# Decode keys of a paged attention turned by VectorE in 32x32 blocks and scored in 16 tiles of the array, with four gate units moved from the prompt's slots to the decode's

## The reference, cut to what matters

```python
s = jnp.einsum('bthd,bnhd->bhtn', q, k_mean)         # block scores (mean key of 256 rows)
_, idx = lax.top_k(s, 3)
s_sel = jnp.einsum('bthd,bhtkld->bhtkl', q, k_sel) * scale
p = softmax(concat([s_sel, s_own]))
out = einsum(p_sel, v_sel) + einsum(p_own, v_own)
u = sigmoid(ga) * (att @ w_attn_br) + sigmoid(gm) * (ml @ w_mlstm_br)
```

## Time and profile before

| | us |
|---|---|
| median of 3 runs (1178.22 to 1182.13) | 1180.7 |
| the profiled execution's own time | 1177.61 |
| its span, first to last instruction | 1175.9 |
| PE busy in the span | 1077.4 (92%) |
| PE weight loads busy | 921.2 (78%) |
| DVE busy | 569.0 (48%) |
| ACT busy | 448.5 (38%) |
| POOL busy | 119.2 (10%) |

### The profile page before, as it was taken

The page is one execution under the profiler, slowest core; times in us unless marked ns, Lnnn a source line. Parts: engine busy times, 40 slices in busy tenths (PEclk is TensorE's granted clock), DMA queues, the critical chain, the costliest instruction groups (busy, mean ns, idle before and its releaser), DMA issues.

```text
span 1175.9 us, 21203 instructions
## 1 busy us (share of the span) xinstructions
PE 1077.4 (92%) x7577; PEld 921.2 (78%) x7577; DVE 569.0 (48%) x1227; ACT 448.5 (38%) x1002; POOL 119.2 (10%) x225
## 2 busy tenths in 40 slices
PE   2999999998999889999989892899999999999993
PEld 2988876887888667777778782898899899889983
DVE  3253524653665565555646427545344334444435
ACT  5154213332554365555543226233133113313312
POOL 2001210220000122333230000000000000000000
PEclk8899989999999999999999997899999999999997
DMA  4432215324114789999974421222222222222312
GB/s 135 141 104 71 54 37 119 80 63 140 50 47 116 259 272 325 339 313 324 314 209 123 160 81 36 72 81 83 81 72 88 80 80 80 84 79 73 96 54 80
DMA packets 93702, 149.81 MB, mean 127 GB/s; under 512 B 9377, under 2 KB 39590, under 8 KB 93622
## 3 DMA queue, kind: packets, MB, share of 16 engines
q1 hardware_dynamic: 75040, 103.83, 29.0%
q0 software_dynamic: 11968, 39.85, 10.0%
q10 hardware_dynamic: 6614, 5.06, 1.5%
HBM read 141.62 MB, written 7.10 MB: 126 GB/s over the span
## 4 chain that ended last, share of the span: by engine, by line
PE 76%; DVE 9%; issue 5%; ACT 4%; DMA 2%; SPq 1%; POOL 1%; ACTq 1%; POOLq 1%; DVEq 0%
PE ps L398 29%; PE ps L423 18%; PE ps L801 8%; PE ps L406 5%; PE ps L1773 4%; PE ps L1814 2%; DMA kring<-in_cache_k_dram 1%; PE ps L1782 1%; PE ps L817 1%; PE ps L877 1%; PE ps L897 1%; ACT w L322 1%; DVE xn L452 1%; PE ps L1212 1%; PE ps L887 1%
## 5 line engine op out<-in xcount | busy, mean ns | idle before, releaser
L333 DVE TENSOR_TENSOR w<-w,w 128x512 fp32r<-128x512 f32 (+1 forms) x256 | 179.7, 706 | 353.5 <-ACT w L322 352.4
L322 ACT ACTIVATE w<-w 128x512 fp32r<-128x512 f32 (+1 forms) x256 | 156.0, 614 | 403.1 <-PE ps L406 233.2
L423 PE MATMUL ps<-h2T,w 128*128 128x288 f32 x1536 | 209.8, 298 | 4.1 <-DVE h2T L511 1.8
L423 PEld LDWEIGHTS ps<-h2T,w 128*128 128x128 f32 x1536 | 207.1, 189 | 6.9 <-DVE wide L2228 2.4
L398 PE MATMUL ps<-w,hid 128*128 128x512 f32 x768 | 184.7, 390 | 0.0
L398 PEld LDWEIGHTS ps<-w,hid 128*128 128x128 f32 x768 | 144.0, 188 | 29.7
L398 PE MATMUL ps<-w,hT 128*128 128x512 f32 x576 | 148.5, 408 | 1.4 <-ACT ri L722 1.4
L398 PEld LDWEIGHTS ps<-w,hT 128*128 128x128 f32 x576 | 108.2, 194 | 27.0 <-issue 4.6
L801 PE MATMUL ps<-hT,w 128*128 128x288 f32 x768 | 125.3, 308 | 0.0
L801 PEld LDWEIGHTS ps<-hT,w 128*128 128x128 f32 x768 | 105.8, 190 | 11.3 <-issue 10.6
L1773 PEld LDWEIGHTS ps<-ident,kring 128*128 128x128 f32 x512 | 56.5, 140 | 41.3 <-DMA kring<-in_cache_k_dram 19.0
(11 more groups left out here) (317 smaller groups left out, 1243.7 us busy)
## 6 DMA issues: line engine op xcount, KB each, us to landing
kring<-in_cache_k_dram SPq DMA_DIRECT2D x128, 256.0 KB, 4.1
vring<-in_cache_v_dram POOLq DMA_DIRECT2D x128, 256.0 KB, 4.6
w<-in_w_in_dram SPq DMA_DIRECT2D x88, 256.0 KB, 2.9
w<-in_w_up_dram SPq DMA_DIRECT2D x64, 256.0 KB, 2.7
w<-in_w_down_dram SPq DMA_DIRECT2D x64, 256.0 KB, 2.6
w<-in_w_out_dram SPq DMA_DIRECT2D x16, 256.0 KB, 2.6
x<-in_x_prompt_dram SPq DMA_DIRECT2D x4, 512.0 KB, 7.0
out_dram<-sC ACTq DMA_DIRECT2D x1, 2048.0 KB
```

The source lines that it names most:

```text
L322: eng.activation(spread(w_hi, n, j, width), together(w32, n, j, width), ACT.Copy)\
L333: eng.tensor_tensor(spread(w_lo, n, j, width), together(w32, n, j, width), spread(w_hi, n, j, width).bitcast(F32), ALU.subtract).then_inc( ...
L423: mm = eng.matmul(ps[:, b, 0:HALFT], w[a][:, j, i * P:(i + 1) * P], right[c][:, k, h * HALFT:(h + 1) * HALFT], start=(k == 0 and (c, a) == ...
```

## The change

1. **Keys.** `keys_turn` on PE and all four copies of a group are gone. In their place DVE turns a whole group with one instruction, `transpose` of [128 x 2048] from `kring` into `kT`, which turns each 32x32 block by itself, at the start of the slot. It waits for the pages and for the scores of the group before; it raises `k_free`.
2. **Scores.** Since a block of 32 partitions of `kT` now holds 32 keys by 32 of the head dimensions, the score is summed over blocks: 64 matmuls of 32 rows x 32 columns against 128 keys for each group, four to each of the 16 tiles (row tile q, column tile h), into banks 2 to 5 (one bank to a row tile), columns 0 to 127. ACT takes them out with two instructions of 256 columns that also accumulate `ssum`; the sum on DVE is gone. The queries for it (`qz`) are laid out by POOL: a memset, then 16 small copies for each sequence; `qz` lies over `gB`.
3. **Probabilities.** They are turned into columns 128 to 255 of the same four banks (before: bank 5), with two more waits: `scores` waits for ACT's copy of the probabilities (`p_PT`), `probs_turn` for ACT's copies of the scores up to the same slot (`p_S`).
4. **Filler.** The prompt's slots have one piece in place of two (17 in all), the decode's slots 15 in 8 slots, and one in each of 33, 35 and 37 (63 in all): 17 pieces, a little over four gate units, are moved, with their weight steps, splits and tanhs.
5. **Queues.** SP: the gates' weight steps come in the order of the slots (`sp_prompt`), the first 8 key pages at slot 12. POOL: the loop of `pool_values` is written out, with the copies of `qz` for sequence b+1 ahead of the value pages of sequence b; `load_g(g_post_mix)` comes after the last scores.

```diff
     def pieces_in(s):
         if s < ALL_GROUPS:
-            return int(s % 8 == 4), 1
-        return (1, 1) if ALL_GROUPS < s <= ALL_GROUPS + 5 else (0, 0)
+            return 1 if s % 8 == 7 else 2
+        return int(s in (33, 35, 37))
...
+    def sp_prompt(eng, n):
+        for r in range(AHEAD + 1):
+            sp_step(eng, n, r)
+        for r in range(NSLOT, AHEAD + NSLOT):
+            sp_step(eng, n, r)
+        for g in range(A_SLOTS):
+            if g == 3 * PT:
+                eng.wait_ge(sem("small_in"), 64)
+                eng.wait_ge(sem("a_kT"), HP)
+                eng.wait_ge(sem("a_qT"), HP)
+                eng.wait_ge(sem("kv_out"), 64)
+                pages(eng, cache_k, kring, "k_in", 0, 0)
+                pages(eng, cache_k, kring, "k_in", 0, 1)
+            for r in fetched_in(g):
+                sp_step(eng, n, r)
...
         def scores(m):
-            eng.wait_ge(sem("p_kT_act"), 2 * m + 2)
-            eng.wait_ge(sem("p_kT_dve"), 2 * m + 2)
-            eng.wait_ge(sem("p_S"), m)
-            for h in range(HP):
-                mm = eng.matmul(ps[32 * h:32 * h + 32, 4, :], qb[:, (m // GROUPS) % 2, h, :], kT[:, h, :],
-                                start=True, stop=True)
+            eng.wait_ge(sem("k_free"), m + 1)
+            eng.wait_ge(sem("p_S"), 2 * m)
+            eng.wait_ge(sem("p_PT"), max(m + 1 - VALS, 0))
+            if m % GROUPS == 0:
+                eng.wait_ge(sem("p_qz"), 16 * (m // GROUPS) + 16)
+            for u, (j, f) in enumerate(((0, 0), (0, 1), (1, 0), (1, 1))):
+                for q in range(4):
+                    r = slice(32 * q, 32 * q + 32)
+                    for h in range(HP):
+                        mm = eng.matmul(ps[32 * h:32 * h + 32, 2 + q, 0:P],
+                                        qz[r, (m // GROUPS) % 2, h, j, f, :], kT[r, :, h, j, f, :],
+                                        start=(u == 0), stop=(u == 3))
...
         def probs_turn(m):
             eng.wait_ge(sem("p_exp"), 2 * m + 2)
             eng.wait_ge(sem("p_PT"), m)
+            eng.wait_ge(sem("p_S"), 2 * min(m + VALS, ALL_GROUPS))
             for j in range(4):
-                mm = eng.transpose(ps[:, 5, j * P:(j + 1) * P], sP[m % 2][:, j * P:(j + 1) * P], ident[:, :])
+                mm = eng.transpose(ps[:, 2 + j, P:2 * P], sP[m % 2][:, j * P:(j + 1) * P], ident[:, :])
...
-            eng.activation(sS[:, g * CH:(g + 1) * CH], ps[:, 4, :], ACT.Copy).then_inc(sem("p_S"), 1)
+            for k in range(2):
+                c = slice(g * CH + k * 2 * PAGE, g * CH + (k + 1) * 2 * PAGE)
+                eng.activation(sS[:, c].rearrange("p (j q n) -> p q j n", j=2, n=32),
+                               ps[:, 2:6, 64 * k:64 * (k + 1)].rearrange("p q (j n) -> p q j n", n=32),
+                               ACT.Copy, accum_out=ssum[:, 2 * g + k:2 * g + k + 1]).then_inc(sem("p_S"), 1)
...
-        def keys(m, h):
-            if h == 1:
-                eng.wait_ge(sem("p_kT_ps"), 3 * m + 2)
-            else:
-                eng.wait_ge(sem("k_free"), m + 1)
+        def keys(m):
+            eng.wait_ge(sem(f"k_in{m % 2}"), 64 * (m // 2) + 64)
             eng.wait_ge(sem("p_S_ps"), m)
-            eng.tensor_copy(kT[:, h, :], ps[:, 3, :]).then_inc(sem("p_kT_dve"), 1)
+            eng.transpose(kT[:, :, :, :, :, :].rearrange("p a h j f n -> p (a h j f n)"),
+                          kring[:, (m % 2) * 4:(m % 2) * 4 + 4, :].rearrange("p a n -> p (a n)"))\
+               .then_inc(sem("k_free"), 1)
...
+    def pool_queries(eng, b):
+
+        if b >= 2:
+            eng.wait_ge(sem("p_S_ps"), GROUPS * (b - 1))
+        for p in range(4):
+            for j in range(2):
+                for f in range(2):
+                    eng.tensor_copy(qz[32 * p:32 * p + 32, b % 2, :, j, f, j * S:(j + 1) * S],
+                                    QTs[64 * j + 32 * f:64 * j + 32 * f + 32, :, b * S:(b + 1) * S])\
+                       .then_inc(sem("p_qz"), 1)
```

More of the change, by code:

```diff
@@ L838, in pe_gates_and_mlstm, with pieces_in, pieces_at, pieces_before @@
                 yield
+    NSLOTS = len(SLOTS)
+    A_SLOTS = NSLOTS + 1
+    A_PIECES = 1
+    GROUPS = NPAGE // 4
+    ALL_GROUPS = B * GROUPS
+    EXPS, VALS = 5, 6
+    DSLOTS = ALL_GROUPS + VALS + 2
+    GATE_PIECES, ML_PIECES = 8 * KT, 2 * KT
+    def pieces_in(s):
+        if s < ALL_GROUPS:
+            return 1 if s % 8 == 7 else 2
+        return int(s in (33, 35, 37))
+    def pieces_at(g):
+        return A_PIECES if g < A_SLOTS else pieces_in(g - A_SLOTS)
+    def pieces_before(g):
+        return sum(pieces_at(t) for t in range(g))
+    def pieces_of(g):
+        return range(pieces_before(g), pieces_before(g + 1)) if g >= 0 else range(0)
+    assert pieces_before(A_SLOTS + DSLOTS) == GATE_PIECES + ML_PIECES
+    def released_by(r):
+        if r < 4 * KT:
+            return 4 * (r // 2) + 2 + r % 2
+        return GATE_PIECES + 2 * (r - 4 * KT) + 1
+    LAST_STEP = 5 * KT + AHEAD
+    def steps_in(g):
+        return [r for r in range(AHEAD, LAST_STEP)
+                if (g == 0 if r < NSLOT else released_by(r - NSLOT) in pieces_of(g - 1))]
+    def fetched_in(g):
+        return [r + NSLOT for r in steps_in(g) if r + NSLOT < LAST_STEP]
     def step_used(eng, step):
@@ L910, in pe_prompt @@
         turn(0, 1)
-        for s in range(NSLOTS + 1):
-            next(main)
-            next(main)
+        for s in range(A_SLOTS):
+            for _ in range(A_PIECES):
+                next(main)
             if s >= 1:
@@ L957, in act_prompt @@
         eng.wait_ge(sem("m_out"), 48)
-        for s in range(NSLOTS + 1):
+        for s in range(A_SLOTS):
+            act_gates(eng, n, s - 1)
             if s >= 1:
-                act_gate(eng, n, (s - 1) // 2, (s - 1) % 2)
                 turned(s - 1)
@@ L1004, in dve_prompt @@
         keys(0)
-        for s in range(NSLOTS + 1):
-            if s >= 1:
-                skip(n, (s - 1) % 2, (s - 1) % 2 == 1)
+        for s in range(A_SLOTS):
+            dve_branches(eng, n, s - 1)
             if s < NSLOTS:
@@ L1760, in pool_values @@
         eng.wait_ge(sem("kv_out"), 64)
-        with eng.Fori(0, B) as b:
+        for b in range(B):
+            if b >= 1 and b + 1 < B:
+                pool_queries(eng, b + 1)
             for g in range(GROUPS):
@@ L1833, in pe_decode @@
         for s in range(DSLOTS):
-            for _ in range(2 * pieces_in(s)[0]):
-                next(main)
             if 1 <= s <= ALL_GROUPS:
                 scores(s - 1)
-            if s < ALL_GROUPS:
-                keys_turn(s, 0)
-                keys_turn(s, 1)
+            for _ in range(pieces_in(s)):
+                next(main)
             if VALS <= s < ALL_GROUPS + VALS:
@@ L1927, in act_decode @@
                 out((s - GROUPS - VALS - 1) // GROUPS)
[L1928 to L1930 removed]
+            for _ in steps_in(A_SLOTS + s):
                 w_high(eng, n)
```

152 lines of the change are left out of this document (49 added, 103 removed).

## The result

The changed kernel takes 1224.3 us (median of 4 runs, 1219.0 to 1226.1) against 1181.4 us for the kernel before (4 runs, 1178.2 to 1183.3): the ratio is 1.036, 95% interval 1.032 to 1.040. It is slower by 43 us where 29 us of gain were predicted. The profiled execution spans 1224.4 us, 48.5 more than before's 1175.9.

The account below looks back on a forecast made before the run. PE was taken to bound the prompt, PE and DMA, 7% apart, slots 6 to 31. Terms -20 + 0 - 5 - 4 = -29 us on the profiled 1177.6 gave 1148.6, 1152 us for the median; range 1138 to 1177.

Parts of the forecast that it names:

- Prompt, -20 (bounds -12 and -29): Prompt attention: seventeen pieces leave, each slot limited by PE alone or its chain, whichever is larger; -20 us.
- Slots 6 to 31, PE's work at 165 us: Decode slots 6 to 31: 171.6 - 49 + 35 + 26 x 0.3 = 165 us of PE work, of 179.3.
- I take 1.3 us: Decode scores: 128 records in 16 tiles take 1.3 us a group, against 1.00 us before.
- 1.9 is free: Decode scores: a burst up to 1.9 us costs nothing; from there PE (181 us) is the limit.
- Issue doesn't forbid it either: Decode scores: a matmul's start takes at most 0.03 us, since eight in column tiles end after 0.25 us.
- my 179: Slots 6 to 31: the stretch stays at 179 us, change 0 us, bounds -4 and +9.
- DVE, 2.3 us a transpose, 122 us in the stretch: Slots 6 to 31: DVE's key transpose takes 2.3 us, bringing DVE to 122 of 179 us.
- POOL, 3 to 5 us of copies, "hidden": Decode: 16 query copies a sequence take 3 to 5 us beside 20 us of page issues, in 27.6 us: hidden.
- DMA, 174 to 187 us: Slots 6 to 31: 59.4 MB take 174 us at 342 GB/s, 177 at share 0.98, 187 at 0.93.
- Slots 0 to 5, -5: Decode slots 0 to 5: from 34.8 to 30 us, -5 us, bounds -8 and 0.
- Last slots, -4: Last slots: seven of ten pieces gone, value pages set 28 to 30 of 33.7 us; -4 us, bounds -8 and 0.
- Sixteen tiles are no faster than four: Rival, decode scores: 3.5 us a burst, PE 223 us in slots 6 to 31, 1213 us in all; chance 0.13.

Follow-up runs that it names:

- filler_only: Kernel before, keys, scores and copies unchanged, with only the 17 filler pieces moved from the prompt's slots to the decode's; 1185.3 us, ratio 1.0035.
- branches_first: Changed kernel, but DVE adds a piece's branch product before it turns the slot's keys, not after; 1203.1 us, ratio 1.020.
- mended: Changed kernel with DVE's branch product before the key turn, neighbouring score matmuls in different row tiles, POOL's query copies two value groups earlier; 1195.7 us, ratio 1.010.
- light_values: mended with only a quarter of each value page loaded after the first two groups, same instructions; 1166.5 us, ratio 0.987.
- half_burst: mended with two of the four score terms left out, 64 records a burst in place of 128; 1148.5 us, ratio 0.974.
- keys_only: Changed kernel's new keys and scores, with the filler pieces where the kernel before had them; 1215.6 us, ratio 1.029.

## Why the prediction was wrong, point by point

- **Prompt, -20 (bounds -12 and -29).** Right in size: -17.3 in the changed kernel and -17.4 in *filler_only*; the stretch is 77.1 us, where I said 74. The reason that I gave holds for one slot in four. The slot of 512 columns takes 5.67 us against 5.6, with 0.98 us of waiting for DVE's division. Those of 384, 256 and 128 take 4.91, 4.50 and 3.38 us against 4.8, 4.3 and 3.2, and in them the profile has PE busy throughout; my sums for PE alone (4.70, 4.06, 3.02) were too low there.

```profile
306.48 0.92 PE L952 MATMUL ps<-KeT,QT 64*128 64x384 f32 x4
...
311.39 0.70 PE L952 MATMUL ps<-KeT,QT 64*128 64x256 f32 x4
...
315.89 0.49 PE L952 MATMUL ps<-KeT,QT 64*128 64x128 f32 x4
...
319.27 1.13 PE L952 MATMUL ps<-KeT,QT 64*128 64x512 f32 x4
...
323.51 0.63 PE L962 MATMUL ps<-ident,pr 128*128 128x128 f32 x4 [0.76 <-DVE pr L1063]
324.35 0.66 PE L962 MATMUL ps<-ident,pr 128*128 128x128 f32 x4 [0.22 <-DVE pr L1063]
```

- **Slots 6 to 31, PE's work at 165 us.** A size was off: "I take 1.3 us" for the scores is 1.84, and the added pieces are 19, not 20 (48 against 29), so the sum becomes 171.6 - 49 + 34 + 26 x 0.84 = 178.4 us, nearly the whole of the stretch before. The rows bear it out: busy time times granted clock is 177.5 us in the changed kernel, 178.7 in *branches_first*, 179.2 in *mended* and 178.1 in *light_values*. My own statement that 1.9 is free was true only if nothing else waits. The reason was the step "Issue doesn't forbid it either": it looked at what a start costs, found nothing that forbids, and did not ask where the instructions come from.
- **What stands on top of 178.4 us** was in no term, and is the step that failed for nearly all of the 67.8 us that the stretch is over my 179: with the burst at its real size alone PE's work would still have fitted. It is stops of instruction supply (18.8 in the row), 18.1 for DVE's product, 7.6 for POOL's copies, and 201.65 - 178.4 = 23 us of PE's own time, the clock at 0.88. Those make 246. The first is shown by the places of the stops, by *half_burst* and by *light_values*, the second by *branches_first*, the third by its going away in *mended*; the clock is read from the rows, and follows PE's idle share of the stretch, if loosely: 0.86 and 0.88 where PE is idle for 18% (*keys_only*, the changed kernel), 0.95 and 0.96 at 13 and 14% (*branches_first*, *mended*), 0.98 and 0.99 at 7 and 8% (*light_values*, *half_burst*).
- **DVE, 2.3 us a transpose, 122 us in the stretch.** Right (2,311 ns, 123.2 us), and still its conclusion was wrong. I counted DVE as no limit by its busy share; its place in the order was what cost. The question to ask was who waits for the instruction behind the transpose.
- **POOL, 3 to 5 us of copies, "hidden".** Their price is right, 0.2 us each. The case that I named, a late copy before a sequence's first scores, happened 4 times for 7.6 us.
- **DMA, 174 to 187 us.** The bytes were right, the best rate too low: in *half_burst*, the one run on this limit, the stretch takes 169.2 us at 349 GB/s, 59.0 MB against my 59.4. It was no limit of the changed kernel.
- **Slots 0 to 5, -5**: +1.9, with the clock at 0.91, the same bursts, and two of the same stops, of 2.0 and 1.3 us. **Last slots, -4**: -0.2. They wait for value pages, and with seven pieces less (PE busy for 20.7 us in place of 28.1) they take the same 33.5 us; the page chain sets them, where I took it for 28 to 30.
- **Rivals.** "Sixteen tiles are no faster than four" had the right sign and size (1213) by another mechanism: 128 columns in 16 tiles take 1.84 us, not 3.5. A slow burst and a late supply of instructions would look alike in the time; only the timeline, 57 records and a gap, tells them apart.

The Trainium skill (TensorE: Matmul & The Clock Gate, Measured speedup vs the span model) led to an estimate of 1.5 us for the burst, nearer to 1.84 than mine. The Trainium skill (TensorEngine Tiling (Array Packing), Instruction Overhead) gives about 60 cycles for each matmul, an estimate of 3.2 us for 128 records; the bursts here run at 12.9 ns a record, half of that, so for tiles of 32x32 the measurement speaks against the figure.

On the supply of instructions the Trainium skill (Runtime: NRT & Kernel Launch, Instruction fetch mechanics) says that each engine refills a small store in blocks of 16 KiB, 256 instructions, by a DMA queue of its own, and that the cost is mostly hidden. The blocks agree with the traces (packets of 16,384 bytes, one more for 256 more instructions of PE, and stops only where a block of 256 begins); "mostly hidden" holds for the kernel before and, but for two stops of 0.6 us, for *half_burst*, and not where 128 records come in 1.64 us beside a DMA share of 0.78 to 0.88. I had not weighed that page.

What stays open: what starts the fetch of a packet, and so why it starts later when DMA is fuller. Where a stop falls is settled by the count of 256, and no kernel changed the fetch alone. Two groups in one burst (256 columns, half as many instructions for each key) might be a mend and weren't tried: `kT` would need 8 KB more in each partition.

## What to carry to other kernels

Before a matmul is cut into many small tiles, count the instructions, not only the columns: here 6,656 more of them for PE, in a decode with a DMA share of 0.78 to 0.88, came with 19 to 32 us of stops of PE that no engine's busy time shows, and the instruction queue and idle time put down to "issue" are the rows to read. Number the engine's instructions in the trace: stops that all fall on one remainder of 256 are stops of supply. An engine at half load is no cover: look at which instruction a new long one is put ahead of, and who waits for it (2.3 us of transpose ahead of one product cost some 20 us, and swapping two lines gave it back). And price each wait on TensorE twice, since the work behind it may run at the lower clock.

## What the runs showed of the hardware that I had not expected

- PE's instructions come by DMA, in packets of 16,384 bytes for 256 of them, on a queue of their own. While a packet is late PE stops in the middle of a run of matmuls whose data is all there, for up to 3.9 us, and always at the same remainder of 256 in its list. The stops inside bursts are gone with 64 records a group in place of 128, and half as long in sum with the DMA share at 0.72 in place of 0.87.
- PE goes on 0.9 us or more after the packet has landed (467 places), and after a stop within 1.1 to 1.6 us.
- 128 records in 16 tiles of 32x32, 128 columns each, take 1.84 us, 12.9 ns a record, and the order of row and column tiles makes no difference. The scores of the same group in four column tiles of 512 columns took 1.00 us.
- DMA moved 349 GB/s over 169 us, above the 342 GB/s of the 20 us that I had taken for the most there is the earlier trace rows.
- After a stop of 2.5 us the next twelve matmuls took 3.19 us in place of 1.85, at a granted clock of 0.53.
